# Key pages turned by VectorE, scores in 32x32 tiles, and a quarter of w_lo made by GpSimd

## The reference

```
kv = rmsnorm(x, kv_norm_w) @ w_kv;  k = rmsnorm(k per head, k_norm_w)
q, g = split(rmsnorm(x, norm_w) @ w_in);  q = rmsnorm(q per head) * 128**-0.5
sample sequence b: keys = 256 cached rows (two pages of 128, by page_table) + its 8 new rows
p = softmax(q . keys + T5 bias by distance);  y = x + (p @ values * silu(g)) @ w_out
```

## Time and profile before

| | us |
|---|---|
| device time, median of 3 runs | 509.81 (509.31 to 509.97) |
| span of the profiled execution, first to last instruction | 508.2 |
| TensorE busy | 502.0 |
| VectorE busy | 352.5 |
| ScalarE busy | 263.2 |
| GpSimd busy | 74.6 |

### The profile page before, as it was taken

The page is one execution under the profiler, slowest core; times in us unless marked ns, Lnnn a source line. Parts: engine busy times, 40 slices in busy tenths (PEclk is TensorE's granted clock), DMA queues, the critical chain, the costliest instruction groups (busy, mean ns, idle before and its releaser), DMA issues.

```text
span 508.2 us, 9171 instructions
## 1 busy us (share of the span) xinstructions
PE 502.0 (99%) x3401; PEld 434.0 (85%) x3401; DVE 352.5 (69%) x651; ACT 263.2 (52%) x532; POOL 74.6 (15%) x85
## 2 busy tenths in 40 slices
PE   7999999999999999999999999999999999999997
PEld 6989978899779978898899999977877778999885
DVE  3865539884789829893598978836756765676662
ACT  5836532574428633464652556945444655655630
POOL 0291004520082102720000240000000000000000
PEclk9999999999999999999999999999999999999999
DMA  8993969999899898999937976526797657684211
GB/s 256 333 349 118 275 245 313 376 358 231 284 343 386 235 277 283 354 328 230 264 103 277 334 244 256 188 83 238 249 326 238 216 171 242 226 309 154 83 53 52
DMA packets 79375, 125.49 MB, mean 247 GB/s; under 512 B 4051, under 2 KB 42148, under 8 KB 79204
## 3 DMA queue, kind: packets, MB, share of 16 engines
q1 hardware_dynamic: 79250, 124.89, 75.4%
q10 hardware_dynamic: 82, 0.02, 0.0%
HBM read 98.93 MB, written 27.57 MB: 249 GB/s over the span
## 4 chain that ended last, share of the span: by engine, by line
PE 95%; DVE 2%; DMA 1%; ACT 1%; issue 1%; SPq 0%; DVEq 0%; ACTq 0%
PE bank L884 45%; PE bank L881 20%; PE bank L865 7%; PE bank L1048 3%; PE bank L993 3%; PE bank L1061 2%; PE bank L1115 1%; PE bank L1007 1%; PE bank L940 1%; PE bank L1161 1%; PE bank L820 1%; PE bank L973 1%; PE bank L974 1%; PE bank L975 1%; DMA eye<-in_c_eye 1%; PE bank L961 1%
## 5 line engine op out<-in xcount | busy, mean ns | idle before, releaser
L1523 DVE TENSOR_TENSOR w_lo<-w_raw,w_hi 128x512 fp32r<-128x512 f32 x207 | 143.8, 733 | 65.7 <-ACT w_hi L1185 65.2
L1185 ACT ACTIVATE w_hi<-w_raw 128x512 fp32r<-128x512 f32 x208 | 118.4, 620 | 58.3 <-PE bank L884 35.0
L884 PE MATMUL bank<-xn_hi,w_hi 128*128 128x320 f32 x320 | 100.1, 317 | 0.7 <-ACT w_hi L1185 0.7
L884 PE MATMUL bank<-xn_hi,w_lo 128*128 128x320 f32 x320 | 97.7, 309 | 0.1
L884 PE MATMUL bank<-xn_lo,w_hi 128*128 128x320 f32 x320 | 97.6, 309 | 0.0
L881 PE MATMUL bank<-w_hi,xn_hi 128*128 128x512 f32 x160 | 65.0, 406 | 0.0
L884 PEld LDWEIGHTS bank<-xn_hi,w_hi 128*128 128x128 f32 x320 | 59.7, 188 | 4.7 <-issue 2.9
L881 PE MATMUL bank<-w_lo,xn_hi 128*128 128x512 f32 x160 | 62.6, 391 | 0.0
L881 PE MATMUL bank<-w_hi,xn_lo 128*128 128x512 f32 x160 | 62.5, 390 | 0.0
L884 PE MATMUL bank<-ym_hi,w_hi 128*128 128x320 f32 x192 | 60.9, 317 | 0.0
L884 PEld LDWEIGHTS bank<-xn_lo,w_hi 128*128 128x128 f32 x320 | 59.8, 188 | 0.4 <-DVE xn_lo L1572 0.2
(11 more groups left out here) (265 smaller groups left out, 766.5 us busy)
## 6 DMA issues: line engine op xcount, KB each, us to landing
w_raw<-in_ret_w_in SPq DMA_DIRECT2D x23, 1024.0 KB, 10.8
st<-in_state_ret SPq DMA_DIRECT2D x32, 512.0 KB, 8.4
out_ret_state_sample<-st SPq DMA_DIRECT2D x32, 512.0 KB, 4.6
w_raw<-in_ret_w_out SPq DMA_DIRECT2D x8, 1024.0 KB, 8.8
w_raw<-in_moba_w_in SPq DMA_DIRECT2D x8, 1024.0 KB, 6.1
cache<-in_cache_k SPq DMA_DIRECT2D x16, 512.0 KB, 4.9
w_raw<-in_w_kv SPq DMA_DIRECT2D x8, 1024.0 KB, 6.4
cache<-in_cache_v SPq DMA_DIRECT2D x16, 512.0 KB, 4.0
```

The costliest lines, as they stand in the source:

```text
L884: mm = pe.matmul(bank[out][:, 0:T], w[:, wk, P * tile:P * tile + P], x[:, k, :], **flags)
L1185: act.activation(w_hi[:, c % 2, part], w_raw[:, c % RAW, part], ACT.Copy).then_inc(w_hi_done, 1)
L1523: dve.tensor_tensor(w_lo[:, c % 2, part], w_raw[:, c % RAW, part], w_hi[:, c % 2, part].bitcast(F32), ALU.subtract).then_inc(w_lo_done, 1)
```

## The change

- KP n is now one VectorE instruction that turns 32x32 blocks of a whole page, straight from the page buffer (keys_turned: ktc for the first sequence of a step, a second buffer ktc2 in scr for the other). TensorE's transposes and both copies go. For this the page is loaded in four DMAs, each a group of 32 partitions (load_page), so that partition group g holds heads 2g and 2g + 1.
- KS q (4 steps for 8) scores two sequences with 64 matmuls of 32x32 weights, in four row groups (by head pair), four column groups and four accumulations e (quarters of the head width), into banks 3, 4, 5, 6 by row group.
- KP stand one by one at places 0 to 3, 6 to 9, 12 to 15, 18 to 21; KS at 5, 11, 17, 23; SE at 12 and 24; KX at 14, 16, 26, 27. SE takes four operations a half, since a row of scores now lies in two banks.
- GpSimd spreads the queries (spread_queries, four copies a head at ME), makes own_q for SN (which takes twice the matmuls), clears part of `wide` after KS 3, and makes the last quarter of w_lo of the four chunks that follow an mk chunk. Bias rows come in 16 DMAs for 8.
- Scores of the second half get buffers of their own (late_ps in scr). SB, PV and the mask are reordered to the new rows of scores, with as many instructions as before.

```diff
-def kp_banks(n):
-
-    return (6, 7) if n % 2 else (3, 4)
+PS_BANKS = (3, 4, 5, 6)
+
+
+def key_page(n):
+
+    q, s, pg = n // 4, n % 4 // 2, n % 2
+    return NPG * (4 * (q // 2) + 2 * s + q % 2) + pg
...
-        if s[0] == "KS" and s[1] % 4 == 0:
-            fill(5, "PS", s[1] // 4)
-        if s[0] == "KP":
-            for b in kp_banks(s[1]):
-                fill(b, *s)
+        if s[0] == "KS" and s[1] % 2 == 0:
+            for b in PS_BANKS:
+                fill(b, "PS", s[1] // 2)
...
-    for n in range(8):
-        at = 2 + 3 * n
-        if n:
-            g[at].append(("KS", n - 1))
-        if n == 4:
-            g[at].append(("SE",))
-        g[at] += [("KP", 2 * n), ("KP", 2 * n + 1)]
-    g[16].append(("KX", 0))
-    g[18].append(("KX", 1))
-    g[26].append(("KS", 7))
+    for n, at in enumerate((0, 1, 2, 3, 6, 7, 8, 9, 12, 13, 14, 15, 18, 19, 20, 21)):
+        g[at].append(("KP", n))
+    for q, at in enumerate((5, 11, 17, 23)):
+        g[at].append(("KS", q))
+    g[12].append(("SE", 0))
+    g[24].append(("SE", 1))
+    g[14].append(("KX", 0))
+    g[16].append(("KX", 1))
...
+        on_pool = [c for c in range(1, nchunks) if chunks[c - 1][0] == "mk"]
+
         def await_lo(eng, c, n):
 
             if c == 0 and n == 3:
                 eng.wait_ge(first_lo_done, 1)
+            elif c in on_pool and n == 3:
+                eng.wait_ge(pool_lo_done, on_pool.index(c) + 1)
             else:
-                eng.wait_ge(w_lo_done, 4 * c + n if c else (2, 1, 3)[n])
-
-        def await_ks(eng, n):
-
-            b = n // 2
-            if n < 0:
-                return
-            if b % 4 == 3:
-                await_full(eng, 5, "PS", b // 4)
+                eng.wait_ge(w_lo_done, 4 * c + n - sum(x < c for x in on_pool) if c else (2, 1, 3)[n])
+
+        def await_ks(eng, q):
+
+            if q % 2:
+                await_full(eng, PS_BANKS[-1], "PS", q // 2)
             else:
-                eng.wait_ge(ks_done, b + 1 - (b + 1) // 4)
+                eng.wait_ge(ks_done, q // 2 + 1)
...
+        def keys_turned(n):
+
+            at = ktc if n % 4 < 2 else ktc2
+            return at[:, n % 2, :, :]
+
+        def scores_at(p):
+
+            return ps[:, p, :] if p < 2 else late_ps[:, p - 2, :]
+
+        def page_loaded(n):
+
+            return 64 * (n // NCP + 1) if n < 16 else 64 * (16 // NCP) + 16 * ((n - 16) // NCP + 1)
...
+                m, vals = (n - 16, True) if n >= 16 else (key_page(n), False)
                 if n >= 16 + NCP:
                     sp.wait_ge(pv_done, n - 15 - NCP)
                 elif n >= NCP:
-                    await_full(sp, kp_banks(n - NCP)[1], "KP", n - NCP)
+                    sp.wait_ge(kt_done, n - NCP + 1)
                 page = sp.value_load(pages[0:1, m:m + 1], min_val=0, max_val=a["cache_k"].shape[0] - 1)
-                src = a["cache_v"] if vals else a["cache_k"]
-                sp.dma_start(cache[:, n % NCP, :], src[bass.ds(page, 1)].rearrange("o p h d -> p (o h d)"))\
-                    .then_inc(cache_loaded[n % NCP], 16)
+                if vals:
+                    sp.dma_start(cache[:, n % NCP, :], a["cache_v"][bass.ds(page, 1)].rearrange("o p h d -> p (o h d)"))\
+                        .then_inc(cache_loaded[n % NCP], 16)
...
+                src = a["cache_k"][bass.ds(page, 1)].rearrange("o (c i) h d -> i (o c) (h d)", i=32)
+                for g in range(4):
+                    sp.dma_start(cache[32 * g:32 * g + 32, n % NCP, :].rearrange("p (c x) -> p c x", c=4), src[:, :, 256 * g:256 * g + 256])\
+                        .then_inc(cache_loaded[n % NCP], 16)
...
+                        for s in range(2):
+                            r0 = 64 * (h % 2) + 32 * s + 16 * (h // 2 % 2)
+                            sp.dma_start(bs[r0:r0 + 16, h // 4, :],
+                                         bass.AP(scratch.tensor, h * LINE + FAR - PAST, [[0, 2], [skew, NEW], [1, PAST + NEW]]))\
+                                .then_inc(bias_loaded, 16)
...
-                elif kind == "KP":
-                    n = step[1]
-                    pe.wait_ge(cache_loaded[n % NCP], 16 * (n // NCP + 1))
-                    for h in range(MH):
-                        b = kp_banks(n)[h // 4]
-                        if h % 4 == 0:
-                            await_free(pe, b, *step)
-                        mm = pe.transpose(bank[b][:, P * (h % 4):P * (h % 4) + P], cache[:, n % NCP, P * h:P * h + P], ident)
-                        if h % 4 == 3:
-                            close(mm, b)
                 elif kind == "KS":
-                    b = step[1]
-                    for n in range(2 * b, 2 * b + 2):
-                        for kp_bank in kp_banks(n):
-                            await_read(pe, kp_bank, "KP", n)
-                    if b % 4 == 0:
-                        await_free(pe, 5, "PS", b // 4)
-                    for half_at in range(2):
-                        for j in range(4):
-                            h = 4 * half_at + j
-                            mm = pe.matmul(bank[5][32 * j:32 * j + 32, PAST * half_at:PAST * half_at + PAST],
-                                           window(2 * h + b // 4, b % 4), ktc[:, :, h, :],
-                                           start=b % 4 == 0 and half_at == 0, stop=b % 4 == 3 and half_at == 1,
-                                           skip_group_check=True)
-                    if b % 4 == 3:
-                        close(mm, 5)
+                    q = step[1]
+                    pe.wait_ge(kt_done, 4 * q + 4)
+                    pe.wait_ge(wide_filled, MH)
+                    if q % 2 == 0:
+                        for b in PS_BANKS:
+                            await_free(pe, b, "PS", q // 2)
+                    last = {}
+                    for e in range(4):
+                        for s in range(2):
+                            at = 32 * (2 * s + q % 2) - NEW * (q % 2)
+                            for h in range(2):
+                                for g in range(4):
+                                    rows_at, c0 = slice(32 * g, 32 * g + 32), 32 * (2 * h + s)
+                                    keys_of = (ktc, ktc2)[s][rows_at, :, 4 * h + e, :]
+                                    last[g] = pe.matmul(bank[PS_BANKS[g]][c0:c0 + 32, 0:PAST], wide[rows_at, 8 * h + 2 * e + q // 2, at:at + 32],
+                                                        keys_of, start=q % 2 == 0 and e == 0, stop=q % 2 == 1 and e == 3,
+                                                        skip_group_check=True)
+                    if q % 2:
+                        for g in range(4):
+                            close(last[g], PS_BANKS[g])
                     else:
-                        mm.then_inc(ks_done, 1)
+                        last[3].then_inc(ks_done, 1)
...
+                    pe.wait_ge(own_q_done, 2)
                     for u in range(4):
-                        for j in range(4):
-                            h, c0 = 4 * (u % 2) + j, TP + 32 * (u // 2)
-                            mm = pe.matmul(bank[4][32 * j:32 * j + 32, TS * u:TS * u + TS], mqT[:, h, c0:c0 + 32], mkT[:, h, TP:T],
-                                           start=True, stop=True)
+                        for x in range(2):
+                            for j in range(4):
+                                h, s = 4 * (u % 2) + 2 * x + j // 2, j % 2
+                                at = P * (h % 4) + TS * (u // 2) + 32 * s
+                                mm = pe.matmul(bank[4][32 * j:32 * j + 32, TS * u:TS * u + TS], own_q[:, u % 2, at:at + 32], mkT[:, h, TP:T],
+                                               start=x == 0, stop=x == 1, skip_group_check=True)
...
-                    if head == 0:
-                        act.wait_ge(wide_cleared, 1)
-                    act.activation(spread[:, 2 * head:2 * head + 2, :, :],
-                                   ps[:, head % 2, TP:T].rearrange("p (g b t) -> p g b t", g=2, t=NEW), ACT.Copy,
-                                   scale=wcols[:, W_Q:W_Q + 1])
...
-                if c >= nchunks:
+                if c >= nchunks or (c in on_pool and n == 3):
...
-                    b = kp_banks(n)[0]
-                    await_full(dve, b, *step)
-                    await_ks(dve, n - 2)
-                    dve.tensor_copy(ktc[:, n % 2, 0:4, :], bank[b][:, :].rearrange("p (h k) -> p h k", h=4))\
-                        .then_inc(bank_read[b], 1)
+                    dve.wait_ge(cache_loaded[n % NCP], page_loaded(n))
+                    if n >= 4:
+                        await_ks(dve, n // 4 - 1)
+                    dve.transpose(keys_turned(n), cache[:, n % NCP, :].rearrange("p (c x j) -> p x c j", c=4, j=32)).then_inc(kt_done, 1)
                 elif kind == "KX":
                     await_full(dve, 6, *step)
                     dve.tensor_copy(mkT[:, 2 * step[1], :], bank[6][:, 0:T]).then_inc(bank_read[6], 1)
```

(63 more changed lines are left out.)

66 lines of the change are left out of this document (34 added, 32 removed).

## The result

The changed kernel takes 516.90 us (median of 4 runs, 515.44 to 517.44) against 509.77 for the kernel before on the same chip: ratio 1.0134, 95% interval 1.0118 to 1.0150. It is 7.1 us slower; the forecast was 507.5 with a range up to 514. The profiled run took 517.44, its span is 515.7.

What follows compares the result with a forecast made beforehand. TensorE, busy 502.0 of 508.2 us, was taken as the bound. Its load falls 13.9 us in the stage, 11.1 become waits for VectorE, 2.8 stay; less 0.5 for GpSimd's copies, 509.81 - 2.3 = 507.5 us, range 501 to 514.

Steps and rivals of the forecast that it cites:

- The walk of the queues: Shared key and value stage, VectorE and TensorE followed in order: 62.8 us for 65.6, with 4.8 us waits before score steps 1 and 3.
- the 1.5 and 0.3 at KX 0 and KX 2: Key column steps: TensorE waits 1.5 and 0.3 us there for the score evacuations on VectorE.
- The turn at 1.13 to 1.22 us: VectorE's turn of one page: 1.22 us alone, 1.13 in a row, taken as 1.15.
- the pages' loads at nothing: SyncE's 64 key DMAs for 16 in the stage: cost 0, or +6 us if the pieces came at two thirds rate.
- ScalarE's part at nothing: ScalarE loses 16 copies and 8 spreads and isn't late anywhere in the stage: 0.
- the end: After mv0 TensorE has the same work and is not waiting for VectorE, so the gain stays.
- (a): During mq, GpSimd's 32 small copies of the queries collide with VectorE's operations: 0.5 us lost (0 to 3).
- (b): GpSimd's quarters of w_lo take 1.30 for 0.68 us each, covered by the scores' waiting: 0.
- 2.8 us won: The stage: 62.8 against 65.6 us; the other 11.1 us of TensorE's gain turn into waiting for VectorE.
- Rival C: TensorE's clock falls after each wait of about 5 us; about 2 us lost, 509.5, no change; chance 20%.
- I take 2.1: Each of four score steps of 64 matmuls takes 2.1 us, sixteen tiles running at once; together 8.4 us.
- rival D: Score steps: 32x32 tiles don't run sixteen at once; 514.5 us with eight, 528.5 with four; chance 15%.

Runs made afterwards that it cites:

- e3_plain_pages: Changed kernel with each key page read by one DMA of whole 4 KB rows instead of four of 1 KB pieces (scores wrongly grouped): 517.32 us.
- e1_busy_gaps: Changed kernel plus 30 matmuls of 320 columns into an unread bank ahead of the waits of score steps 1 and 3: 513.72 us.
- e2_shift: Changed kernel plus 30 matmuls of 32 columns ahead of score step 1 only: 514.82 us.
- e5_between_40: Changed kernel with new stage order, later table load, sooner page loads and 20 small matmuls (40 records) before the first two key column steps: 508.53 us.
- e1_tb_late: Changed kernel with the 1 MB load for the queries' table issued five places later in SyncE's order: 513.37 us.
- e2_half_keys: Changed kernel with three of every four score matmuls reading 128 key columns instead of 256 (scores incomplete): 516.95 us, one run.

## Why the prediction was wrong

**The walk of the queues held for its two long waits.** It had 4.8 us before steps 1 and 3; the trace has 5.66 and 4.85, and 4.96 and 4.88 in the run with plain page loads. That the sums agree too, 11.3 for 11.4, is in part luck: the 1.5 and 0.3 at KX 0 and KX 2 are not in the trace, and 0.78 before step 2 is. The turn at 1.13 to 1.22 us (1.24), the pages' loads at nothing (e3_plain_pages), ScalarE's part at nothing (the trace has no new wait for it) and the end were right: of the stage's 8.7 us and mk0's start 0.9 sooner 7.8 are left, and the span grew by 7.5. (a), 0.5 us lost ahead of the stage, is not to be seen: mk0 starts at 330.12 in the first profile and at 329.91 to 332.00 in the others in which GpSimd copies the queries, at 331.03 and 330.79 in the two in which it doesn't. (b) at nothing may be low by about 2 us; it is not well measured, and nothing in the kernel before.

**The step that failed is the sum, "2.8 us won": it let a wait cost its length.** Rival C had the mechanism and a fifth of the chance; it has happened behind every stop. It was priced at 1.8 us a step, of which 1.5 was to be hidden by the wait at KX 0, so 2 in all; the trace has 1.8 and 1.3 in the two steps with nothing hidden, since that wait didn't come, 0.5 in the projections behind step 1, and 1.7 behind a third stop that the forecast didn't have: 5.3. That the clock is the cause of the slow step is shown by filling the wait: 3.9 us with the small matmuls at 0.50, 2.4 with the wide ones at 1.00.

By the Trainium skill, page "TensorE: Matmul & The Clock Gate", Part 1, a TensorE that has idled falls to 1.2 GHz. The trace agrees: 0.50 behind three stops of 4.0 to 5.7 us, and 1.00 behind the one filled with wide matmuls.

**No term stood for the arrival of TensorE's own instructions.** The change puts 288 more records, each with its load, into the stream and packs them at 0.02 us a record. A piece of some 250 loads and matmuls then arrives late: 4.0 us, and the 1.7 of clock behind it. Shown by the count (34 records for 16), by the spacing (124 records), by the number of packets, by the packet that ends 1.3 to 1.8 us before each of the 13 stalls does, and by what takes the stall away: more records ahead (e1_busy_gaps, e2_shift, e5_between_40) or, down to 1.3 us, less traffic (e1_tb_late). Why a packet comes late in one order and not in another stays open.

**"I take 2.1" for a step was 0.6 low** (2.69, the point at which rival D turns the sign), but in e2_half_keys a step of 2.04 took nothing off the time, so the 2.4 us in the account above can't be had back by the step alone. That is one run, with a stall of 4.4 us in it. D was the wrong rival to give the far side of the range to.

By the trace's account the stall and the clock are 9.3 of the 11.5 us by which the stage missed; the runs take both away, but no run prices each alone. With the order, the loads and the seam put right the same change goes from 516.9 to 507.4. That this is the forecast is luck: the walk's waits are then smaller, and other waits have come.

## What to carry to other kernels

An idle stop of 4 to 5 us on TensorE was paid twice here, its length and the low clock behind it; price it so, or fill it. When many small matmuls replace few large ones, count instructions as well as columns, and look for waits on "issue" inside a run of them; if there is one, try a few more instructions ahead of it before changing anything else, and look at when the instruction queue's packets come. A second engine that looks 60% busy over a stage has to be walked in order, instruction by instruction.

## What the runs showed of the hardware

- TensorE's program arrives in packets of 16 KB, one for 250 to 254 loads and matmuls (27, 29 and 30 packets for 6802, 7378 and 7498); two stalls in one trace stand 124 of each apart. A seam cost 1.3 to 5.7 us where its packet was late, with the DMA engines at a share of 1.0 to 1.2, and nothing where it was in (e5_between_40, 6.5 us ahead). TensorE went on 1.3 to 1.8 us behind the packet's end.
- 32x32 tiles with 256 columns each: in the changed kernel's step 0 the first 32 records start in 0.46 us (338.85 to 339.31), the other 96 take 2.23 us up to the first projection, 0.023 each; with 128 columns (e2_half_keys) 0.017. The Trainium skill, page "TensorE: Matmul & The Clock Gate", Part 3, gives some 4 ns of issue for each further tile. Here the first 32 records, each with a new weight, start 14 ns apart, and the measurement decides; the 23 ns that follow depend on the columns and hold more than issue.
- A turn of 128x1024 fp32 by VectorE in 32x32 blocks is 1.24 us, 2.37 for two in a row, so the second adds 1.13 for its 1024 elements a lane.
